# Modulation vectors and the beta/decay projection on four column groups of TensorE

## What is computed

```python
# first block (c, c_ctx), second block twice (c_2, c_ctx_2): modulation vectors
sh1, sc1, gt1, sh2, sc2, gt2 = split(silu(c) @ w_mod + b_mod, 6)      # w_mod: 1024 x 6144
csh1, csc1, ...              = split(silu(c_ctx) @ w_mod + b_mod, 6)
sh_x, sc_x, g_x              = split(silu(c_2) @ mod_w[i] + mod_b[i], 3)   # i = 0, 1; 1024 x 3072
# mixer of the first block: u = h @ w_in, of which 16 columns are ba
beta = sigmoid(ba[:, :, :, 0])                      # 2 directions x 4 heads
g = -exp(a_log) * softplus(ba[:, :, :, 1] + dt_bias)
o_f, o_b = gated delta rule over the tokens, both directions, with beta and g
```

## Time and profile before

| | |
|---|---|
| median of 3 runs | 2943.22 us (2941.11 to 2945.61) |
| the profiled execution, first to last instruction | 2943.6 us |
| TensorE busy with matmuls | 2529.8 us (86%), 19642 records |
| VectorE, ScalarE, GpSimd busy | 1355.8, 706.8, 459.3 us |
| line 246 (parts), busy: first block, dispatch and router, read-out | 54.9, 23.9, 22.9 us |
| line 559 (`ba`), from first start to last end | 10.48 us |

### The profile page before, as it was taken

One profiled execution on the slowest core, in us unless ns is written; L12 is line 12 of the kernel. 1 busy time (PEld: TensorE's weight loads), 2 busy tenths in 40 slices (PEclk: granted clock), 3 DMA queues, 4 the chain that ended last, 5 costly groups with the idle time before them and its releaser, 6 DMA issues. The chain is left out here.

```text
span 2943.6 us, 48528 instructions
## 1 busy us (share of the span) xinstructions
PE 2529.8 (86%) x19642; PEld 1482.2 (50%) x19642; DVE 1355.8 (46%) x2690; ACT 706.8 (24%) x1271; POOL 459.3 (16%) x426
## 2 busy tenths in 40 slices
PE   5999864988899999996189999979998499989988
PEld 3553443954444444342145566458887145455553
DVE  1650646533511111111887885966665571034442
ACT  3111440102111111110325541133333113134441
POOL 0000132300111111111000000032221220034550
PEclk8999876998999999999599999999999799999999
DMA  6110600016489999995616545245443932021001
GB/s 250 52 58 5 226 19 20 7 58 221 175 356 394 389 416 410 390 390 210 251 31 175 147 127 174 111 133 137 127 128 78 358 117 95 6 40 18 15 29 65
DMA packets 328930, 471.43 MB, mean 160 GB/s; under 512 B 151465, under 2 KB 225107, under 8 KB 304005
## 3 DMA queue, kind: packets, MB, share of 16 engines
q1 hardware_dynamic: 302645, 373.92, 36.8%
q10 hardware_dynamic: 12960, 69.21, 5.8%
q0 software_dynamic: 13104, 25.19, 2.3%
HBM read 413.82 MB, written 76.55 MB: 167 GB/s over the span
## 5 line engine op out<-in xcount | busy, mean ns | idle before, releaser
L1953 PE MATMUL psum<-ex_w,hT 128*64 128x512 f32 (+1 forms) x1104 | 329.8, 618 | 26.2 <-DMA ex_w<-in_exp_w_up 24.4
L1953 PEld LDWEIGHTS psum<-ex_w,hT 128*64 128x64 f32 (+1 forms) x1104 | 125.6, 158 | 224.4 <-issue 222.4
L3996 POOL TENSOR_SCALAR mla_pool<-mla_pool,at_stats 128x768 f32<-128x768 f32 x64 | 140.2, 2203 | 252.4 <-DVE at_stats L4014 252.4
L2186 DVE COPY slot_act_t<-psum 128x256 f32<-128x256 f32 x45 | 19.1, 424 | 325.8 <-PE psum L1961 325.8
L551 PE MATMUL psum<-hT,weights 128*128 128x512 f32 x384 | 166.8, 592 | 0.0
L1969 PE MATMUL psum<-ex_w,slot_act_t 128*64 128x512 f32 (+1 forms) x552 | 163.4, 597 | 1.4 <-DVE slot_act_t L2186 1.4
L1938 POOL DMA_INDIRECT scratch_ys<-slot_out,slot_row x45 | 45.3, 1006 | 465.9 <-issue 402.8
L551 PEld LDWEIGHTS psum<-hT,weights 128*128 128x128 f32 x384 | 73.0, 190 | 86.7 <-issue 86.1
L2142 ACT ACTIVATE slot_silu<-psum 128x256 f32<-128x256 f32 x45 | 17.3, 384 | 398.2 <-PE psum L1953 398.2
L3170 PE MATMUL psum<-rs_r_ident,rs_b 64*32 64x96 f32 x1536 | 84.4, 249 | 13.1 <-POOL rs_k_ident L3142 12.8
L3894 PE MATMUL psum<-mla_kT,at_qT 128*128 128x512 f32 (+1 forms) x256 | 93.3, 489 | 2.6 <-DVE at_qT L4006 1.6
(11 more groups left out here) (595 smaller groups left out, 4955.8 us busy)
## 6 DMA issues: line engine op xcount, KB each, us to landing
ex_w<-in_exp_w_gate SPq DMA_DIRECT2D x64, 1024.0 KB, 9.3
ex_w<-in_exp_w_up SPq DMA_DIRECT2D x64, 1024.0 KB, 19.0
ex_w<-in_exp_w_down ACTq DMA_DIRECT2D x60, 1024.0 KB, 10.3
mod_ring<-in_w_mod SPq DMA_DIRECT2D x12, 2048.0 KB, 12.6
scratch_features<-tokens SPq DMA_DIRECT2D x96, 256.0 KB, 3.9
weights<-in_w_in SPq DMA_DIRECT2D x6, 2048.0 KB, 8.2
ex_w<-in_mod_w SPq DMA_DIRECT2D x6, 2048.0 KB, 12.4
ex_w<-scratch_ys SPq DMA_DIRECT2D x8, 1536.0 KB, 19.0
```

The costliest lines, as they stand in the source:

```text
L1953: mm = pe.matmul(bank[at:at + n, :], XT[:, k, at:at + n], W[:, 0:2, k * DE:(k + 1) * DE], start=(k == 0), stop=(k == KD - 1))
L3996: pool.tensor_scalar(Pm[:, q % 2, u, :], Pm[:, q % 2, u, :], st[:, 3, u:u + 1], None, ALU.mult)\
```

## The change

A part's matmuls take 32 columns of the padded vectors instead of 64 and go in turn to four groups of 32 array columns (PSUM partitions 0, 32, 64 and 96). The copy out, the bias and the sum stay; the sum's constant now picks rows 0 and 1 of each 32. For `ba`, the six token tiles are dealt to the four groups: group 0 takes tiles 0 and 4, group 1 tiles 1 and 5, groups 2 and 3 one tile each, all in bank 0. The stationary operand has 32 columns of which 16 count. `baT` becomes 128 x 256, the copies out become 128x128 and 64x128, and two transposes take the place of six.

```diff
--- before.py
+++ after.py
@@ -145,7 +145,7 @@
     out[:, MIX_COL + 4:SLOT_COL] = (s_ // HD == t_ // HD)
     out[:, SLOT_COL:TOKEN_COL] = np.arange(NE) * HOME
     out[:, TOKEN_COL:SUM_COL] = np.arange(SUM_COL - TOKEN_COL) * P + t[:, None]
-    out[:, SUM_COL:CONST_COLS] = t[:, None] % 64 == np.arange(2)[None, :]
+    out[:, SUM_COL:CONST_COLS] = t[:, None] % RC == np.arange(2)[None, :]
     s, u = t[:, None] % RC, np.arange(RC)[None, :]
     for d in range(2):
         at = PAIR_COL + d * (LANE_COL - PAIR_COL) // 2
@@ -242,9 +242,9 @@
         if c:
             pe.wait_ge(self.S["m_evac"], c)
         for k in range(KD):
-            at = 64 * (k % 2)
-            mm = pe.matmul(self.K.bank[self.parts][at:at + 64, :], self.items[c][0][:, k, :],
-                           self.ring[:, c % RING, k, :], start=(k < 2), stop=(k >= KD - 2))
+            at = RC * (k % 4)
+            mm = pe.matmul(self.K.bank[self.parts][at:at + RC, :], self.items[c][0][:, k, 0:RC],
+                           self.ring[:, c % RING, k, :], start=(k < 4), stop=(k >= KD - 4))
         mm.then_inc(self.S["m_part"], 1)
 
     def evac(self, act, c):
@@ -519,7 +519,7 @@
     with ExitStack() as c, phase(nc, names, W) as (block, S):
         w_in = (S["w_in0"], S["w_in1"], S["w_in2"])
         U = c.enter_context(sbuf(nc, "conv_in", [P, NU, UC + UX], F32))
-        baT = c.enter_context(sbuf(nc, "baT", [16, TT], F32))
+        baT = c.enter_context(sbuf(nc, "baT", [P, 2 * P], F32))
         PAD = TAPS // 2
         n_plain = NCF * 3
 
@@ -554,14 +554,16 @@
             n = len(loads) - 1
             pe.wait_ge(w_in[n % RING], 16 * (n // RING + 1))
             pe.wait_ge(S["plain_out"], n_plain)
-            for b0, t0, t1 in ((0, 0, TC), (1, TC, TT)):
-                for k in range(KD):
-                    mm = pe.matmul(K.bank[b0][0:16, 0:t1 - t0], K.wring[:, n % RING, k, 0:16], K.hT[:, k, t0:t1],
-                                   start=(k == 0), stop=(k == KD - 1))
+            for k in range(KD):
+                tiles = K.hT[:, k, :].rearrange("p (j t) -> p j t", t=P)
+                for g in range(4):
+                    mm = pe.matmul(K.bank[0][g * RC:(g + 1) * RC, 0:P * len(range(g, NT, 4))]
+                                   .rearrange("p (j t) -> p j t", t=P), K.wring[:, n % RING, k, 0:RC],
+                                   tiles[:, g::4, :], start=(k == 0), stop=(k == KD - 1))
             mm.then_inc(S["mm_x"], 1)
             pe.wait_ge(S["plain_out"], n_plain + 2)
-            for j in range(NT):
-                tr = pe.transpose(K.bank[2][:, j * 16:(j + 1) * 16], baT[:, j * P:(j + 1) * P], K.ident[0:16, 0:16])
+            pe.transpose(K.bank[2][:, 0:P], baT[:, 0:P], K.ident[:, :])
+            tr = pe.transpose(K.bank[2][:, P:P + 2 * RC], baT[0:2 * RC, P:2 * P], K.ident[0:2 * RC, 0:2 * RC])
             tr.then_inc(S["ba_turned"], 1)
 
         @block.gpsimd
@@ -597,8 +599,8 @@
                 dst, func = ((zT, ACT.Silu), (cfa, ACT.Copy), (cfs, ACT.Sigmoid))[which]
                 act.activation(dst[:, q, :], K.bank[2 * (f % 4)][:, :], func).then_inc(S["plain_out"], 1)
             act.wait_ge(S["mm_x"], NQKV + n_plain + 1)
-            act.activation(baT[:, 0:TC], K.bank[0][0:16, 0:TC], ACT.Copy).then_inc(S["plain_out"], 1)
-            act.activation(baT[:, TC:TT], K.bank[1][0:16, :], ACT.Copy).then_inc(S["plain_out"], 1)
+            act.activation(baT[:, 0:P], K.bank[0][:, 0:P], ACT.Copy).then_inc(S["plain_out"], 1)
+            act.activation(baT[0:2 * RC, P:2 * P], K.bank[0][0:2 * RC, P:2 * P], ACT.Copy).then_inc(S["plain_out"], 1)
 
         @block.vector
         def _(dve):
@@ -620,7 +622,8 @@
                                                            op0=ALU.mult, op1=ALU.add)
                         ins.then_inc(done if tap == TAPS - 1 else tap_done[seg], 1)
             dve.wait_ge(S["ba_turned"], 1)
-            dve.tensor_copy(ba, K.bank[2][:, 0:NT * 16].rearrange("p (j n) -> p j n", n=16)).then_inc(S["ba_out"], 1)
+            dve.tensor_copy(ba, K.bank[2][:, 0:NT * RC].rearrange("p (j n) -> p j n", n=RC)[:, :, 0:16])\
+                .then_inc(S["ba_out"], 1)
 
 
 def between(K, I, vecs, C, Ktok, Vtok, ba, G):
```

## The result

The changed kernel takes 2922.25 us (median of 5 runs, 2918.0 to 2932.36) against 2943.22 (5 runs, 2941.11 to 2946.57): a ratio of 0.993 with a 95% interval of 0.991 to 0.995, or 21 us less. The forecast was 2919.4 in a range of 2912 to 2932. In a later set of runs the same kernel took 2920.33 (5 runs) against 2942.95 (23 runs), ratio 0.9933 (0.9919 to 0.9946).

The account below looks back on a forecast made before the run. No single engine was taken to bound the kernel; an edit is worth what its phase loses at its end. 7.4 + 8.6 + 1.6 + 1.5 + 3.0 + 1.7 = 23.8 us less: 2919.4 us, range 2912 to 2932.

Parts of the forecast that it names:

- Four groups at once: In each part, four column groups work at once: 1.93 us instead of 3.65, 1.72 us gained at full clock.
- (b): Only two groups work at a time, so parts cost what they did and `ba` gains: 2937.5 us; chance 0.08.
- (c): Narrow groups run one after another, a part takes 7.1 us and the kernel gets slower: 2991 us; chance 0.04.
- Mixer: End of the mixer's projections: `ba` matmuls 6.9 us less, gap 0.35, transposes 0.15, counted in full: -7.4 us.
- Read-out: Six parts; the first gains nothing, five in TensorE's gapless list gain 1.72 us each: -8.6 us.
- rival (d): VectorE becomes the bound of the read-out and its five parts give half: 2923.7 us; chance 0.06.
- Stages that wait for loads: Opening -1.6, conformer -1.5, between -3.0, router and dispatch -1.7 us; parts there begin when their loads land.
- opening: Only the last part counts, mostly at half clock, and the small matmuls stay slow: -1.6 us, bounds -1.0 and -2.2.
- between: Two parts: the first's copy starts 2.4 us earlier, the second gives 1.7 if the clock is up: -3.0 us.
- conformer stage: Two parts give 2.6 us at full clock, of which a lower clock could take 2 back: -1.5 us.
- router and dispatch: Only each phase's last part gains, 3.4 us together, or nothing with the clock down: -1.7 us taken.
- Rival (a): Clock falls between loads; conformer, router, dispatch, half of between give nothing, conformer and dispatch cost 2 each: 2928.7 us; chance 0.12.

Follow-up runs that it names:

- parts_twice: The kernel after with every part's eight matmuls issued twice in a row, the second time over the first: 2943.26 us, ratio 0.9991 to the kernel before.
- ba_only: The kernel before with only beta and decay on four groups: 2945.81 us, ratio 0.9992; in a second set 2940.56 us, ratio 1.0005.
- old_ba_twice: The kernel before with the 16 matmuls of beta and decay (line 559) issued a second time over the first: 2960.31 us, ratio 1.006.

## Why the prediction was right, and where it was not

**Four groups at once** held to the hundredth: the part was forecast at 1.93 us and takes 1.92, and at the lower clock 3.65 and 3.64. What the scan's rows suggested for 64 rows by 32 columns holds for 128 rows. Rivals (b) and (c) fall by that row alone.

**Mixer.** Line 560 was forecast at 3.59 us and takes 3.65, the gap 0.6 and takes 0.56, the transposes 0.4 and take 0.54, as before: -7.2 for -7.4. The step "nothing is beside this chain, so it counts in full" is the weak one. It is so in the stage, in each of nine traces. In the time it counted 4 to 9 us by medians where the parts were new (2929.24 and 2929.07 against 2920.33 to 2924.84), 2.4 to 3.8 us by the ratios of the same runs, and nothing where the parts were old (ratios 0.9992 and 1.0005). Two sets of 12 runs and `parts_twice` (0.9991), whose mixer was 7.2 us shorter as well, point the same way, but only the interval of the second set leaves the 7.2 us out; the other two reach down to 0.9975 and 0.9974. Why it is so is open. The traces exclude a wait of a later stage for `ba`. The granted clock of the timed runs gives a hint: in the mean it was 0.9278 and 0.9289 in the two sets of `ba_only`, against 0.9295 and 0.9303 in the runs of before beside them, and 0.9280 against 0.9299 for `old_ba_twice`, which lost 6 us more than its stage. Among runs of the kernel before alone, 0.001 less clock went with 1.2 to 2.6 us more, so these differences would make 2 to 5 us (an estimate). `parts_twice`, with 0.9297 against 0.9295, does not fit. Where in the kernel the clock falls, and whether beta and decay make it fall, is not shown.

**Read-out.** Forecast -8.6, seen -8.5 in the mean, by the period of 17.5 that was forecast at 17.6. VectorE stayed off the path; rival (d) falls.

**Stages that wait for loads.** Forecast -7.8 in all, seen -11.7. All were mis-sized to the same side, for the most part by one term: at which clock the last parts and the lists behind them run. In the opening the small matmuls of line 283 were taken to stay slow (5.96 us); they took 4.92 us in one execution and 6.98 in the other, and the stage went to 56 or to 59. In between the forecast took 3.0 of bounds of 0.9 and 4.1, and the mean is 4.6, beyond the better bound. The second part ran at full clock in four of six executions. In four, too, the matmuls with the selector at the end took 1.95 us, where they took 2.5 to 3.2 with the old parts; the sum had not counted them. The conformer stage gave 2.4 of its 2.6, router and dispatch 2.4 of 3.4.

**Rival (a), the clock.** Its mechanism was seen: the clock comes down between loads (0.74 from 290 to 319, parts at 3.54 and 3.64 us). Its price was for the most part not: it would have left the conformer stage no gain, and this stage gave nearly all. What counts is which part is slow. An early one may end 1.7 us later, since the next load lands only 5.4 us after the last (296.34, 301.75). The last one, on which the end hangs, comes behind full work (line 881) and ran at full clock in each execution with the new parts. Between them stands the part ahead of the sums over the convolution. It was slow in the first profile of the kernel after (313.35) and fast in the second; the rows that follow it are, first profile first:

```profile
316.76 1.91 PE L270 MATMUL psum<-mod_sums,const 128*2 128x512 f32 x2
318.61 3.87 PE L872 MATMUL psum<-cf_conv,const 128*128 128x512 f32 x8
322.41 1.98 PE L877 MATMUL psum<-mod_row,row_selector 2*128 2x512 f32 x4
```

```profile
317.62 1.02 PE L270 MATMUL psum<-mod_sums,const 128*2 128x512 f32 x2
318.57 3.86 PE L872 MATMUL psum<-cf_conv,const 128*128 128x512 f32 x8
322.36 1.98 PE L877 MATMUL psum<-mod_row,row_selector 2*128 2x512 f32 x4
```

Counted from the start of the stage (279.92 and 282.19), line 877 begins after 42.5 and 40.2 us, and after 40.1 to 40.4 in the other kernels with the new code. So the lower clock cost 2.3 us at this place once in the six executions without extra work: about the size that the rival gave it, but seldom. The rule of the Trainium skill (TensorE: Matmul & The Clock Gate, "Loop structure matters more than you think") describes the clock's row rightly and says nothing on who waits for the slower part.

**The sum.** The forecast 23.8 us off the profile became 24.8 in the first pair of profiles and 21.0 by medians. That agreement is better than the terms deserve: the stages would give 27.4, and the kernel shows 21 to 23. Part of the difference may be the open point on beta and decay. The rest of the kernel, outside the seven stages, moves as well: it took 2263.8 us in the profile of before, 2268.1 and 2263.6 in those of the kernel after, and 2258 to 2270 over all fourteen, and no experiment tells whether that is chance or comes from the change.

## What to carry to other kernels

A matmul with few stationary columns can be dealt along its contraction or along its tokens to four groups of 32 columns, and then took about half of the time that two groups took here (1.92 for 3.65 us), and about a third of that on one group where the groups were unequal (3.65 for 10.48 us); what it brings is TensorE's time, so count only places where TensorE's list has no gap or where a chain to the stage's end hangs on it. The order of issue between the groups did not matter for a list of eight matmuls. Below some 0.3% a single pair of profiles misleads in this kernel, in both directions: price an edit by the rows of its own stage, take the time from many runs, and do not expect the two to agree to a few microseconds.

## What was not expected of the hardware

- Column groups start without regard to the order of issue: 1.95 us with each group's two matmuls back to back, 1.92 with them in turn. The semaphore on the last matmul issued still came behind all of them (its record ended at 277.58, the last of the other groups at 278.19, ScalarE began at 278.26).
- Four groups of 128 rows by 32 columns with 512 float32 columns each overlap whole: 16 records of 592 ns in 1.92 us, 32 in 3.64.
- The same 64 matmuls of 128 x 64 took 7.33 us in one execution and 12.95 in another, both times in a list without a gap and without a wait for a load; with the stretch around it the granted clock was 1.00 and 0.74.
- Extra work that keeps the clock up between loads (0.88 instead of 0.74) made its own stages hardly shorter, about 0.5 us of 175; in both executions with it, a later list took 5.40 us instead of 3.70.
